# HGRN2 mixer of a fused block: the next head's gate, scan, differences and first factors moved into the present head, the loop written out, and TensorE's filler products spread evenly

## The reference

```python
q, f, i, gate = split(u @ w_in)
log_f = logaddexp(log(lb), log1p(-lb) + log_sigmoid(f))
k = (1.0 - lb) * sigmoid(-f)
# per head: S_t = diag(f_t) S_{t-1} + k_t v_t^T,   o_t = S_t^T q_t   (q through silu)
y = head_rms_norm(o, norm_gain) * silu(gate)
return y @ w_out
```

## Time and profile before

| | us |
|---|---|
| median of 3 runs (1871.11 to 1876.53) | 1874.06 |
| the profiled execution: time | 1869.55 |
| its span | 1867.6 |
| TensorE busy (share of the span) | 1748.8 (94%) |
| VectorE busy | 1090.0 (58%) |
| ScalarE busy | 849.7 (45%) |
| GpSimd busy | 421.5 (23%) |
| mean granted TensorE clock | 0.983 |

### The profile page before, as it was taken

The page is one execution under the profiler, slowest core; times in us unless marked ns, Lnnn a source line. Parts: engine busy times, 40 slices in busy tenths (PEclk is TensorE's granted clock), DMA queues, the critical chain, the costliest instruction groups (busy, mean ns, idle before and its releaser), DMA issues. The chain is left out here.

```text
span 1867.6 us, 24306 instructions
## 1 busy us (share of the span) xinstructions
PE 1748.8 (94%) x8346; PEld 1396.8 (75%) x8346; DVE 1090.0 (58%) x1676; ACT 849.7 (45%) x1450; POOL 421.5 (23%) x332
## 2 busy tenths in 40 slices
PE   7997999999999999889999799999999989899997
PEld 5666887877888888777877687888888866666665
DVE  5544454467656643676777748756553387667343
ACT  5553555554333332546545635433332353444563
POOL 0341554211111100133553440111100012222222
PEclk9998999999999999999999999999999999999999
DMA  5111100232232223212121112232322221211121
GB/s 203 37 68 57 46 35 23 74 108 77 93 101 90 95 96 101 90 57 68 45 67 57 55 46 85 85 101 91 100 90 101 93 79 46 79 46 46 57 68 45
DMA packets 39892, 140.12 MB, mean 75 GB/s; under 512 B 4496, under 2 KB 4752, under 8 KB 39696
## 3 DMA queue, kind: packets, MB, share of 16 engines
q1 hardware_dynamic: 39824, 139.23, 21.9%
HBM read 137.11 MB, written 2.10 MB: 75 GB/s over the span
## 5 line engine op out<-in xcount | busy, mean ns | idle before, releaser
L187 PE MATMUL bank<-u_high,w_high 128*128 128x512 f32 x1580 | 653.3, 413 | 29.3 <-POOL w_low L160 10.8
L189 PE MATMUL bank<-u_high,w_low 128*128 128x512 f32 x1580 | 623.1, 394 | 0.0
L188 PE MATMUL bank<-u_low,w_high 128*128 128x512 f32 x1580 | 623.0, 394 | 0.0
L187 PEld LDWEIGHTS bank<-u_high,w_high 128*128 128x128 f32 x1580 | 301.3, 191 | 117.1 <-issue 40.9
L189 PEld LDWEIGHTS bank<-u_high,w_low 128*128 128x128 f32 x1580 | 300.5, 190 | 65.5
L188 PEld LDWEIGHTS bank<-u_low,w_high 128*128 128x128 f32 x1580 | 301.5, 191 | 57.7 <-issue 4.1
L151 ACT ACTIVATE w_high<-w_ring 128x1024 fp32r<-128x1024 f32 x233 | 243.4, 1052 | 222.1 <-PE bank L189 171.7
L160 DVE TENSOR_TENSOR w_low<-w_ring,w_high 128x1024 fp32r<-128x1024 f32 x176 | 220.5, 1259 | 188.4 <-ACT w_high L151 185.2
L160 POOL TENSOR_TENSOR w_low<-w_ring,w_high 128x1024 fp32r<-128x1024 f32 x57 | 135.7, 2388 | 512.6 <-ACT w_high L151 512.6
L881 ACT ACTIVATE conv_up<-bank,col_sb 128x512 f32<-128x512 f32 x88 | 68.5, 779 | 270.6 <-DVE bank L936 270.6
L996 POOL TENSOR_TENSOR hidden<-conv_up 128x512 f32 x44 | 58.2, 1322 | 494.1 <-DVE conv_up L947 373.8
(11 more groups left out here) (405 smaller groups left out, 2313.1 us busy)
## 6 DMA issues: line engine op xcount, KB each, us to landing
w_ring<-ffn_up SPq DMA_DIRECT2D x88, 512.0 KB, 3.2
w_ring<-ffn_down SPq DMA_DIRECT2D x44, 512.0 KB, 3.2
w_ring<-c_in SPq DMA_DIRECT2D x32, 512.0 KB, 3.3
w_ring<-g_in SPq DMA_DIRECT2D x16, 512.0 KB, 3.7
w_ring<-m_in SPq DMA_DIRECT2D x12, 512.0 KB, 5.0
w_ring<-fox_in SPq DMA_DIRECT2D x12, 512.0 KB, 3.4
w_ring<-dsa_in SPq DMA_DIRECT2D x12, 512.0 KB, 3.2
w_ring<-ab_out SPq DMA_DIRECT2D x8, 512.0 KB, 4.1
```

Source lines behind the costliest of these rows:

```text
L187: nc.tensor.matmul(out, a[0], b[0], start=start, stop=False)
L188: nc.tensor.matmul(out, a[0], b[1], start=False, stop=False)
L189: return nc.tensor.matmul(out, a[1], b[0], start=False, stop=stop)
```

## The change

It touches `hgrn2` alone. All loops over heads become Python loops, so every instruction stands once per head in the code. Within head h:

- VectorE takes v and makes the diagonal first, then merges level after level. Between merges, one task each: the output of head h - 1 (`out`), the low parts, the clamp, and after merge 4 the keys and q of head h + 1, after merge 5 its scan and difference 0, after merge 6 its differences 1 to 3. State, last difference, low parts and g follow.
- ScalarE makes the logarithm, silu and first four exponentials of head h + 1 inside head h; the root of h - 1 comes at the start of h.
- GpSimd makes kd and qd, the factors 4 to 6 of h and the factors 0 to 3 of h + 1.
- TensorE starts a head with x0, then the norm matmul of head h - 1 (now in the bank of the states), then fills: in heads 1 to 6 three products after x0, after each level and after the state product, one after the transposes, four at the end. Head 0 has 16 products ahead of x0, three behind it, one in each gap and four at the end. The last head has its 28 output products after the levels and around the state.

```diff
+    slots_first = [16, 19, 20, 21, 22, 23, 24, 25, 26, 27, 28, 32]
+    slots_next = [0, 3, 6, 9, 12, 15, 18, 21, 24, 25, 28, 32]
+    slots_last = [0, 0, 3, 6, 9, 12, 15, 18, 21, 23, 25, 28]
+    def freed(h, l):
+        if l >= R:
+            return h, l - R
+        return h - 1, (l + R if l + R < NL else l)
...
+            def fill(h, n):
+                if h == 0:
+                    project(1, slots_first[n], slots_first[n + 1])
+                elif h < H - 1:
+                    project(h + 1, slots_next[n], slots_next[n + 1])
+                else:
+                    mix(slots_last[n], slots_last[n + 1])
...
+            def core(h):
+                if h == 0:
+                    project(1, 0, slots_first[0])
+                pe.wait_ge(q_ready, h + 1)
+                pe.wait_ge(diff_ready, x_at(h, 0))
                 for c in range(NT):
                     ins = nc.tensor.matmul(b_x0[:, c * P:(c + 1) * P], kk[:, c * P:(c + 1) * P], q[:, c * P:(c + 1) * P], start=True, stop=True)
                 ins.then_inc(lv_done, 1)
+                if h:
+                    norm(h - 1)
+                fill(h, 0)
+                pe.wait_ge(raw_ready, h + 1)
+                k.turn(b_v, vraw).then_inc(v_turned, 1)
                 for l in range(NL):
                     level(h, l)
+                    fill(h, l + 1)
...
+            def silu_q(h):
+                act.wait_ge(q_taken, h + 1)
+                if h:
+                    act.wait_ge(lv_done, 8 * (h - 1) + 1)
+                    act.wait_ge(x_ready, NL * h)
+                nc.scalar.activation(q[:, :], qraw[:, :], ACT.Silu).then_inc(q_ready, 1)
...
+            def step(h):
+                if h:
+                    root(h - 1)
+                values(h)
+                high(h + 1, 3)
+                exps(h, 4)
+                exps(h, 5)
+                high(h + 2, 0)
+                exps(h, 6)
+                early(h + 1)
+                log(h + 1)
+                silu_q(h + 1)
+                silu_gate(h)
+                nc.scalar.preload_act_table_set(LNEXP)
+                exps(h + 1, 0)
+                turned_keys(h)
+                high(h + 2, 1)
+                exps(h + 1, 1)
+                exps(h + 1, 2)
+                exps(h + 1, 3)
+                decay_keys(h + 1)
+                high(h + 2, 2)
+                decay(h + 1)
+                output(h)
...
+            def step(h):
+                pool.wait_ge(kdf_ready, h + 1)
+                nc.gpsimd.tensor_tensor(kd[:, :], kk[:, :], kdf[:, :], ALU.mult).then_inc(kd_ready, 1)
                 pool.wait_ge(e_ready, h + 1)
+                if h:
+                    pool.wait_ge(o_done, h)
                 nc.gpsimd.tensor_tensor(qd[:, :], q[:, :], E[:, :], ALU.mult).then_inc(qd_ready, 1)
+                for l in range(R, NL):
+                    factor(h, l)
+                if h < H - 1:
+                    for l in range(R):
+                        factor(h + 1, l)
...
+            def merge(h, l):
+                dve.wait_ge(lv_done, 8 * h + l + 2)
+                dve.wait_ge(at_done, 8 * h + l + 1)
+                if l + R < NL:
+                    diff(h, l + R)
+                else:
+                    nc.vector.memset(tick[:, l + R - NL:l + R + 1 - NL], 0.0)
+                nc.vector.copy_predicated(chunks(at), mask("levels", l * P).bitcast(U32), chunks(b_x[(l + 1) % 2])).then_inc(at_done, 1)
...
+            def step(h):
+                diagonal(h)
+                merge(h, 0)
+                if h:
+                    out(h - 1)
+                merge(h, 1)
+                low(h + 1, 3)
+                merge(h, 2)
+                clamp(h + 1)
+                merge(h, 3)
+                low(h + 2, 0)
+                merge(h, 4)
+                keys(h + 1)
+                take_q(h + 1)
+                merge(h, 5)
+                scan(h + 1)
+                diff(h + 1, 0)
+                merge(h, 6)
+                for l in range(1, R):
+                    diff(h + 1, l)
+                state(h)
+                decay_keys(h + 1)
+                low(h + 2, 1)
+                take_g(h + 1)
+                low(h + 2, 2)
...
             clamp(0)
+            take_q(0)
+            take_g(0)
             low(1, 2)
+            keys(0)
+            scan(0)
+            for l in range(R):
+                diff(0, l)
+            decay_keys(0)
+            for h in range(H - 1):
+                step(h)
+            last_step(H - 1)
             half.low(dve, KD - 1)
```

More of the change, by code:

```diff
@@ L1084, in level, with norm @@
                 ins.then_inc(lv_done, 1)
[L1086 to L1108, removed]
+            def norm(h):
+                pe.wait_ge(osq_ready, h + 1)
+                nc.tensor.matmul(b_kv[:, :], k.c("ones"), k.sq[:, 0, :], start=True, stop=True).then_inc(nrm_done, 1)
+            def core(h):
[3 more added lines that the diff above has]
+                pe.wait_ge(diff_ready, x_at(h, 0))
                 for c in range(NT):
@@ L1149, in core @@
                 ins.then_inc(o_done, 1)
[L1150 to L1166, removed]
-            core(H - 1, False, False)
+                fill(h, 10)
+            for h in range(H):
+                core(h)
+            norm(H - 1)
+            half.tile(pe, 4, (4, 5, 7))
+            pe.wait_ge(rs_ready, H)
+            half.tile(pe, 4, (6,)).then_inc(k.proj_done, 1)
+            half.tile(pe, 5, range(4, KD)).then_inc(k.proj_done, 1)
         @block.scalar
@@ L1259, in _ @@
+            for l in range(R):
+                factor(0, l)
+            for h in range(H):
                 step(h)
@@ L1298, in step, with scan @@
-                for l in range(R):
-                    diff(h, l)
-                nc.vector.tensor_tensor(chunks(kdf), chunks(G), chunks(G)[:, :, P - 1:P].to_broadcast([P, NT, P]), ALU.subtract).then_inc(g_ready, 1)
-                if not nxt:
-                    half.low(dve, 0)
+            def scan(h):
+                dve.wait_ge(logf_ready, h + 1)
+                if h:
+                    dve.wait_ge(e_ready, h)
+                ch.link(nc.vector.tensor_tensor_scan(G[:, :], k.c("reset"), logf[:, :], 0.0, ALU.mult, ALU.add))
@@ new lines, in last_step @@
+            def last_step(h):
+                diagonal(h)
+                half.low(dve, 0)
+                merge(h, 0)
+                half.low(dve, 1)
+                out(h - 1)
+                merge(h, 1)
+                half.low(dve, 2)
+                merge(h, 2)
+                half.low(dve, 3)
+                merge(h, 3)
+                half.low(dve, 4)
+                low(h + 1, 3)
+                merge(h, 4)
+                half.low(dve, 5)
+                merge(h, 5)
+                half.low(dve, 6)
+                merge(h, 6)
+                state(h)
+                out(h)
```

264 lines of the change are left out of this document (135 added, 129 removed).

## The result

The changed kernel takes **1845.11 us** (median of 4 runs, 1842.87 to 1847.34); the kernel before, in runs of the same chip, 1872.59 (4 runs, 1870.77 to 1876.53). The ratio is 0.985, 95% interval 0.9827 to 0.9873. That is 27.5 us less, where the sum had 25.1: faster, and inside the range of 1843 to 1859. The profiled execution took 1843.4 us. The single number that was forecast, 1849.0, is 3.9 us away; 1.5 of that is the kernel before, whose median over four runs is 1872.59 where three gave 1874.06.

What follows compares the result with a forecast made beforehand. TensorE was taken to bound the phase, with gains where it stands still. Start -0.4, head 0 -7.1, heads 1 to 6 -13.6 and last head -4.0 sum to -25.1: from 1874.06 to 1849.0 us, range 1843 to 1859.

Steps and rivals of the forecast that it cites:

- the sum: All terms of the phase together, start to last head: 25.1 us less, giving 1849.0 from the median.
- Heads 1 to 6: With the new order each head takes 33.5 us (bounds 33.0 and 34.6), six take 201.0 instead of 214.6: -13.6.
- the written layout: One head of 1 to 6 timed from level 0 for each engine: scan and difference 0 to 19.9, state 24.3.
- The turned keys: In heads 1 to 6 TensorE waits for them before the state product: 0.2 at least, up to 1.5, taken as 0.5.
- Rival A: VectorE or ScalarE slips 1 us at keys and turned keys in each head: 34.7 a head, +7.2, 1856; 20%.
- Head 0: Takes 29.4 us against 36.54, -7.1, with 8.2 of new waits against 21.2 of work; bounds 6 and 10.
- rival B: After head 0's 4.3 us wait the levels run at 1.2 GHz, ten microseconds costing about 4: 1853; 12%.
- The last head: Nothing waits for the gate; x0 to norm takes 30.4 us against 34.42: -4.0, the slow clock and two waits.
- GpSimd beside VectorE: Their queues must overlap 10.1 us a head; at least 7.6 already do, so the lock rule cannot hold for all.
- Rival D: In the six heads VectorE and GpSimd take turns and VectorE's queue bounds; at 38.3 a head, 1877.7; 3%.
- Rival E: Code written out seven times stalls the queues' fetch; a stall of 4 us a head gives 1873; 2%.
- Rival C: No wait in the six heads, a shorter one in head 0: 33.0 each and 27.5, 1844; 8%.

Runs made afterwards that it cites:

- even-fills run: The kernel before with only TensorE's fillers spread evenly, the gate still made inside its own head: 1878.91 us, ratio 1.0041.
- Merges first: Tested by a run of the changed kernel with VectorE's tasks, output to keys and q, each one place earlier, ahead of a merge: 1846.99 us, ratio 0.9869.
- late-gate run: The changed kernel with most of the last head's gate (keys, q, scan, first differences) made at its own start again: 1851.99 us, ratio 0.9901.

## Why the prediction was right

**The bound and the gain: right.** TensorE bounds the phase, and what it gained is where it stood. The even-fills run adds what the prediction did not have: that the present head's gate closes a loop, so this spread of fills without the early gate loses 7 us instead of gaining. The early gate without even fills loses far more. "Merges first" carries nothing in heads 1 to 6. No run has the loops written out and nothing else changed; the prediction's zero for that, with 0.5 a head on either side, fits heads of 33.27 and isn't shown by itself.

**Heads 1 to 6: right, 33.27 for 33.5.** No merge is waited for, the state neither. Head 1 in VectorE's timeline (columns as in the earlier trace rows), laid beside the written layout:

```profile
850.55 0.69 DVE L1354 TENSOR_TENSOR c_dif<-c_G 128x512 f32<-128x512 f32 x1 [3.59 <-PE bank L1116]
...
865.98 1.21 DVE L1392 TENSOR_TENSOR_SCAN c_G<-cst_sb,c_logf 128x512 f32<-128x512 f32 x1
867.22 0.69 DVE L1354 TENSOR_TENSOR c_dif<-c_G 128x512 f32<-128x512 f32 x1
868.30 0.75 DVE L1406 COPY_PREDICATED c_attn<-cst_sb,bank 128x512 f32<-128x512 uint32 x1 [0.39 <-issue]
868.93 3.25 DVE L1354 TENSOR_TENSOR c_dif<-c_G 128x512 f32<-128x512 f32 x3
872.27 0.29 DVE L1416 COPY c_S<-bank 128x128 f32<-128x128 f32 x1
```

I take level 0 at 849.26, one spacing of 2.95 ahead of the level at 852.21 (its first load is recorded at 849.35), so the scan is at 16.7 (layout 17.8), and the state ends 24.1 behind level 0 (layout 24.3). The order of the work is what was written, about a microsecond early in its middle.

**The turned keys: the size nearly, the reason wrong.** The term was 0.5 "because the queue is as full as its table loads allow", against 0.3 measured. ScalarE in head 1:

```profile
867.16 1.28 ACT L1255 ACT_TABLE_LOAD   x1
868.46 0.44 ACT L1209 ACTIVATE c_dif<-c_dif 128x256 f32<-128x256 f32 x1
868.80 0.43 ACT L1210 ACTIVATE c_dif<-c_dif 128x256 f32<-128x256 f32 x1
870.68 0.49 ACT L1232 ACTIVATE c_kdt<-bank 128x384 f32<-128x384 f32 x1 [1.46 <-PE bank L1144]
```

The queue is free 1.46 us before the transposes are there: its exponentials end at 20.0 behind level 0 (869.23 - 849.26), where the layout had 20.95. The copy starts at 21.4 and the state product at 21.97; the layout had the keys ready at 21.95, and 0.2 of wait. The step that failed is the one that raised these 0.2 to 0.5, and up to 1.5, for a full queue. The wait is the way from the transposes through the copy and back against one product of cover, the same in each head, and worth less than a third of itself when taken away. Rival A lived on this queue and did not come.

**Head 0: the waits right, 28.54 for 29.4 in part by luck.** The long wait stands before the state product, 3.96 for 4.3, behind the next head's first exponentials. Levels 4 to 6 wait for merges, as laid out: 2.44 in all for some 2.9. The 1.0 before the output, for the state, did not come; no such wait is recorded. So the waits are 6.4 us for the 8.2 of the sum. The turned keys are ready at 21.3 behind x0 (837.72) where the layout had 22.7. Half a microsecond of that is given back from there to x0 of head 1, 7.2 instead of 6.7, because state product and output run at 1.2 GHz. In the two later profiles the state product starts 21.2 behind x0 and 8.0 to 8.1 us follow, 29.3 in all: closer to 29.4, but as the sum of a layout 1.4 us too long and a clock that it had at nothing. That is **rival B**, which came in part: for some 3.6 to 5 us at 1.2 GHz behind the wait and not for ten, and on the state product and output instead of the levels.

```profile
839.94 1.18 PEld L1156 LDWEIGHTS bank<-c_attn,c_v 128*128 128x128 f32 x4
841.00 0.49 PEld L1161 LDWEIGHTS bank<-c_qd,c_S 128*128 128x128 f32 x2
841.41 0.30 PEld L1156 LDWEIGHTS bank<-c_attn,c_v 128*128 128x128 f32 x2
```

Four loads of the output take 1.18 (0.64 in head 1), the next pairs 0.49 and then 0.30: in this profile the clock is back within 4 us of the state product's start. In the second profile of the kernel the pairs still take 0.55 up to 841.16, 4.7 us behind that start.

**The last head: right, 30.64 for 30.4**, with no wait above 0.3. That the gate made late is what brings wait and slow clock there, the late-gate run shows.

**GpSimd beside VectorE: right that it costs nothing here, wrong in the reason.** The records of the two in heads 1 to 5 of the changed kernel add up to 224.6 us in 166.37, so they overlap for at least 11.6 us a head; the prediction asked for 10.1. Groups of VectorE, then of GpSimd, in head 1 of the changed kernel (columns as in the earlier trace rows):

```profile
L1354 DVE TENSOR_TENSOR c_dif<-c_G 128x512 f32<-128x512 f32 x7 | 7.1, 1032 | 3.6 <-PE bank L1116 3.6
L160 DVE TENSOR_TENSOR w_low<-w_ring,w_high 128x1024 fp32r<-128x1024 f32 x4 | 5.5, 1380 | 0.0
```

```profile
L1320 POOL TENSOR_TENSOR c_X<-c_q,c_dif 128x256 f32<-128x256 f32 x8 | 10.2, 1277 | 0.0
L1324 POOL TENSOR_TENSOR c_kd<-c_k,c_kdf 128x512 f32<-128x512 f32 x1 | 1.3, 1280 | 0.0
```

A difference costs 1.03 instead of 0.93 and a factor 1.28 instead of 1.18, but the decay product only 1.28 instead of 2.26. Over the whole program VectorE's busy time is what it was, 1090.1 for 1090.0, and GpSimd's is 8.3 us more. They slow each other in new places and spare each other in old ones. Rival D would have needed VectorE's queue to be the bound; it stands 3.6 us in front of each head's first merge.

The step that failed is the one that took overlapping records for work done side by side. Where they overlap the records are longer. Shortest, median and longest (ns) of a difference and of a factor's second operation in heads 1 to 5:

```profile
L1354 DVE TENSOR_TENSOR c_dif<-c_G x35: 669/1196/1368, 850.6 to 1004.0; 128x512 f32<-128x512 f32 x35
L1320 POOL TENSOR_TENSOR c_X<-c_q,c_dif x36: 712/1190/1771, 843.4 to 1009.8; 128x256 f32<-128x256 f32 x36
```

By the starts and ends of these heads' records, VectorE's operations with two inputs in SBUF overlap GpSimd's for 55.9 us in all, and those operations and GpSimd's together are 46.5 us longer than if each were as short as the shortest of its line. So much of the overlap can be one waiting for the other. The rule of the Trainium skill (SBUF — State Buffer, "Who interferes with whom"), that the shared port pair is an exclusive lock, fits these durations and is not refuted by the overlap, against what the prediction says. It costs this change nothing that shows, because TensorE bounds and both queues have room; these runs do not tell which pairs take turns.

**The rest.** Rival E fell: no long wait of a queue came with the written-out code, and the instruction queue moved 49 packets where it was 41. Rival C had 1844 and the median is 1845.11, but it was to come from a head of 33.0 and a head 0 of 27.5, and neither is there. The forecast's sum was 2.2 us too small in the phase: 1.4 in the six heads, 0.9 in head 0, 0.1 at the start, less 0.2 in the last head. Of these only the six heads and the last one repeat; in the two later profiles the clock takes 1.6 us at the start and 0.8 in head 0, and their phase of 271.95 meets the forecast's 271.8 by that chance. Outside of it, the two profiles differ by 1.2 us, less than profiles of one kernel do.

## What to carry to other kernels

Before filling the bounding engine's gaps evenly, follow the chain that runs through them and see whether it closes on itself from one iteration to the next; if so, the fills lengthen it, and its head must first be moved into the iteration before. The two are then one change: here each was slower than the kernel before when it was run alone. An early gate also pays at seams: there a wait of TensorE of 4.2 us brought 3.3 us more behind it, in slow clock and smaller waits.

## What the runs showed of the hardware that was not expected

Two profiles of the same program differ by some 6 us of 1840 outside the phase that was edited, and three by 2.4 us inside it, and over all kernels here the rest of the program took 1566.5 to 1577.5 us. In the rows above TensorE was busy for 87.35 and 87.37 us of the same hundred but granted 0.95 and 0.90. A single profile therefore can't confirm a gain of a few microseconds by its span. The stretch that was edited can, where it repeats: heads 2 to 6 took 33.23 to 33.35 in all three profiles of the changed kernel, but the start and head 0 took 39.34 in one and 41.7 in two.

And "idle before" is not all time to be won: a wait of 0.32 us of a weight load, repeated in each head, gave 0.09 when it was removed.

The releaser that a profile names for a wait can be wrong: three levels of head 0 start 0.12 us behind a merge, and one of them is put down to an X that had been ready for 1.8 us.
